# First attention of a three-part transformer kernel: fp32r scores, the bias added on VectorE, tables by sixteen small DMAs, and a value product moved behind two score jobs

## What is computed

```python
s_own = einsum('hqd,hkd->hqk', qm, k_own) * scale + tb_moba[:, rel_bucket(d_own)]
p     = masked_softmax(s_own, d_own >= 0)              # 8 heads
s_cmp = einsum('gjqd,gnd->gjqn', qn, k_cmp) * scale + tb_nsa[:, :, rel_bucket(d_cmp)]
s_s   = einsum('gjqd,gqnkd->gjqnk', qn, k_s) * scale + tb_nsa[...]   # selected
s_w   = einsum('gjqd,gkd->gjqk', qn, k_w) * scale + tb_nsa[...]      # window
o_b   = g0 * softmax(s_cmp) v_cmp + g1 * softmax(s_s) v_s + g2 * softmax(s_w) v_w
```

## Time and profile before

| | us |
|---|---|
| median of the timed runs (1383.39 to 1383.76) | 1383.43 |
| the profiled execution's own time | 1381.03 |
| its span, first to last instruction | 1379.2 |
| PE busy in the span | 1317.9 (96%) |
| DVE busy | 793.6 (58%) |
| ACT busy | 617.5 (45%) |
| POOL busy | 173.1 (13%) |
| mean granted clock of TensorE, share of full speed | 0.971 |

### The profile page before, as it was taken

One profiled execution on the slowest core, in us unless ns is written; L12 is line 12 of the kernel. 1 busy time (PEld: TensorE's weight loads), 2 busy tenths in 40 slices (PEclk: granted clock), 3 DMA queues, 4 the chain that ended last, 5 costly groups with the idle time before them and its releaser, 6 DMA issues.

```text
span 1379.2 us, 23104 instructions
## 1 busy us (share of the span) xinstructions
PE 1317.9 (96%) x9908; PEld 1226.2 (89%) x9908; DVE 793.6 (58%) x1062; ACT 617.5 (45%) x936; POOL 173.1 (13%) x224
## 2 busy tenths in 40 slices
PE   5999999999999999999999999998799888999997
PEld 5997669999999868999999999998797558999996
DVE  5745446555456465556454766547755765766643
ACT  5424445554333354554345444444544534544432
POOL 4000002110000001111011111010402401011101
PEclk8999999999999999999999999999999959999999
DMA  6571004555636502455544454563252006255461
GB/s 253 215 248 61 1 31 148 183 183 191 206 132 205 187 7 92 156 183 205 194 160 167 163 184 163 189 207 142 94 201 69 1 1 221 94 187 182 146 208 71
DMA packets 33494, 204.45 MB, mean 148 GB/s; under 512 B 3552, under 2 KB 5872, under 8 KB 13168
## 3 DMA queue, kind: packets, MB, share of 16 engines
q1 hardware_dynamic: 33392, 202.97, 42.8%
HBM read 201.89 MB, written 1.07 MB: 147 GB/s over the span
## 4 chain that ended last, share of the span: by engine, by line
PE 83%; DVE 7%; issue 6%; ACT 3%; POOL 1%; DMA 0%; SPq 0%; POOLq 0%; ACTq 0%; DVEq 0%
PE ps L614 22%; PE ps L615 22%; PE ps L616 22%; PE ps L884 3%; DVE wl L567 2%; PE ps L635 1%; PE ps L636 1%; PE ps L637 1%; PE ps L885 1%; PE ps L836 1%; PE ps L1280 1%; PE ps L1278 1%; POOL acc L699 1%; PE ps L2189 1%; ACT wh L559 1%
## 5 line engine op out<-in xcount | busy, mean ns | idle before, releaser
L567 DVE TENSOR_TENSOR wl<-raw,wh 128x2048 fp32r<-128x2048 f32 (+3 forms) x201 | 429.1, 2139 | 212.5 <-ACT wh L559 212.2
L614 PE MATMUL ps<-xh,wh 128*128 128x256 f32 x1712 | 492.1, 287 | 34.4 <-DVE xl L689 17.2
L615 PE MATMUL ps<-xl,wh 128*128 128x256 f32 x1712 | 489.8, 286 | 0.0
L616 PE MATMUL ps<-xh,wl 128*128 128x256 f32 x1712 | 489.5, 286 | 0.0
L559 ACT ACTIVATE wh<-raw 128x2048 fp32r<-128x2048 f32 (+3 forms) x201 | 357.3, 1782 | 208.6 <-PE ps L616 179.2
L614 PEld LDWEIGHTS ps<-xh,wh 128*128 128x128 f32 x1712 | 334.5, 195 | 37.3 <-issue 25.1
L615 PEld LDWEIGHTS ps<-xl,wh 128*128 128x128 f32 x1712 | 334.4, 195 | 0.0
L616 PEld LDWEIGHTS ps<-xh,wl 128*128 128x128 f32 x1712 | 334.2, 195 | 0.0
L614 PE MATMUL ps<-ah,wh 128*128 128x256 f32 x1088 | 309.6, 285 | 1.1 <-DVE wl L567 1.1
L615 PE MATMUL ps<-al,wh 128*128 128x256 f32 x1088 | 308.8, 284 | 0.0
L616 PE MATMUL ps<-ah,wl 128*128 128x256 f32 x1088 | 308.7, 284 | 0.0
(11 more groups left out here) (323 smaller groups left out, 1314.5 us busy)
## 6 DMA issues: line engine op xcount, KB each, us to landing
raw<-wstream SPq DMA_DIRECT2D x157, 1024.0 KB, 4.9
raw<-wstream SPq DMA_DIRECT2D x32, 704.0 KB, 4.1
raw<-wstream SPq DMA_DIRECT2D x8, 768.0 KB, 4.2
e_bt<-scratch SPq DMA_DIRECT2D x4, 512.0 KB, 6.6
raw<-wstream SPq DMA_DIRECT2D x2, 560.0 KB, 5.5
consts<-consts SPq DMA_DIRECT2D x1, 1025.0 KB, 9.9
raw<-wstream SPq DMA_DIRECT2D x4, 256.0 KB, 5.2
h<-xt SPq DMA_DIRECT2D x4, 256.0 KB, 5.8
```

The lines of the kernel that those rows point to most:

```text
L567: e.g.tensor_tensor(WL[q][:, 0:w], RAW[i % RAWN][:, 0:w], f32(WH[q][:, 0:w]), ALU.subtract).then_inc(S["lo"], 1)
L614: e.g.matmul(o, wh[:, sl], xh[:, cs], start=start, stop=False, skip_group_check=pair)
L615: e.g.matmul(o, wh[:, sl], xl[:, cs], start=False, stop=False, skip_group_check=pair)
L616: ins = e.g.matmul(o, wl[:, sl], xh[:, cs], start=False, stop=k == p.nk - 1, skip_group_check=pair)
```

## The change

- **Scores.** Queries and keys get the high and low fp32r halves that the weights have. VectorE drains a pair to fp32, ScalarE rounds it (`act_halves`), VectorE subtracts (`dve_low`), for seven pairs of 128x512. A score block becomes three fp32r matmuls for the first 128 queries and three for the second.
- **Bias.** The products with `flip` go. VectorE adds the table with a `tensor_tensor_reduce` that reads the scores in PSUM and the table in SBUF, writes the negated sum to `PB` and reduces it by the minimum (`dve_max_biased`); ScalarE's exponential reads `PB` (`act_exp_biased`). The scores of job i wait for the maximum of job i-3 instead of its exponentials. The compressed scores are fp32r products of 16 columns, and VectorE adds their bias.
- **Tables.** The row is written 16 times for each head (16x16x385 in DRAM), and sixteen DMAs of 16 partitions and eight heads each read it in the right order of queries: eight behind the query product `qn`, eight behind `ev0`.
- **Order.** The value product `ev1`, with its drains, and VectorE's gates and compressed weights (`dve_even_gates`) go behind the first two score jobs, on PE, ACT and DVE.

```diff
+        def dve_halves(p, full, dh, dl, at, n, by=None):
+            product = dve_to(p, full, n, by)
+            def drain(e, pair):
+                if pair:
+                    dve_low(e, full, dh, dl, at, pair - 1)
+                product(e, pair)
+            return drain
+        def dve_low(e, full, dh, dl, at, pair):
+            sl = slice(pair * 512, pair * 512 + 512)
+            e.wait_ge(S["qkh"], at + pair + 1)
+            e.g.tensor_tensor(dl[:, sl], full[:, sl], f32(dh[:, sl]), ALU.subtract).then_inc(S["qkl"], 1)
+        def act_halves(p, full, dh):
+            def drain(e, pair):
+                sl = slice(pair * 512, pair * 512 + 512)
+                e.wait(p.out[pair])
+                e.g.activation(dh[:, sl], full[:, sl], ACT.Copy).then_inc(S["qkh"], 1)
+            return drain
...
+        def dve_max_biased(e, A, i, first, second):
+            b, p = A.bank(i), PB[i % 4]
+            e.wait_ge(S["sc"], A.base + i + 1)
+            if i >= 4:
+                e.wait_ge(S["tp"], A.pv(i - 4) + 1)
+            e.g.tensor_tensor_reduce(p[:, 0:128], PS[b][:, 0:128], first, -1.0, 3e38, ALU.add, ALU.min, nm(i)[:, 0:1])
+            e.g.tensor_tensor_reduce(p[:, 128:384], PS[b][:, 128:384], second, -1.0, 3e38, ALU.add, ALU.min,
+                                     nm(i)[:, 1:2]).then_inc(S["mx"], 1)
...
+            for a in range(8):
+                src = bass.AP(scratch.tensor, 8 * half * 16 * 385 + 127 - 16 * a, [[384, 16], [16 * 385, 8], [1, 256]])
+                e.g.dma_start(e_bt[16 * a:16 * a + 16, hs].rearrange("p (h s) -> p h s", h=8), src).then_inc(S[f"bt{half}"], 16)
...
-            act_gemm(e, G["km"])
+            act_gemm(e, G["km"], drain=act_halves(G["km"], e_kmf, e_kmh))
...
-            dve_gemm(e, G["km"], 0, drain=dve_to(G["km"], e_km, 0))
+            dve_gemm(e, G["km"], 0, drain=dve_halves(G["km"], e_kmf, e_kmh, e_kml, 2, 0))
             for i, name in enumerate(("cmpk", "cmpv")):
                 p = G[name]
                 dve_gemm(e, p, 0)
+                if i == 0:
+                    dve_low(e, e_kmf, e_kmh, e_kml, 2, 1)
...
+            A = EVEN
+            for i in range(A.n + 4):
+                if i == 2:
+                    dve_even_gates(e)
...
-            pe_toks(e, G["ev1"], x_ready(0))
             A = EVEN
             for i in range(A.n + 3):
+                if i == 2:
+                    pe_toks(e, G["ev1"], x_ready(0))
...
+        def pe_even_scores(e, i):
+            A = EVEN
+            if i == 0:
+                e.wait_ge(S["row"], 1)
+                e.wait_ge(S["qkl"], 7)
+            if i >= 3:
+                e.wait_ge(S["mx"], i - 3 + 1)
...
+            for o, s, n in ((ps[:, 0:128], qt * T, 128), (ps[:, 128:384], qt * T + 128, 256)):
+                qs, ks = slice(s, s + 128), slice(kt * T, kt * T + n)
+                e.g.matmul(o, qh[p_, qs], kh[p_, ks], start=True, stop=False)
+                e.g.matmul(o, qh[p_, qs], kl[p_, ks], start=False, stop=False)
+                ins = e.g.matmul(o, ql[p_, qs], kh[p_, ks], start=False, stop=True)
+            ins.then_inc(S["sc"], 1)
```

More of the change, by code:

```diff
@@ L430, in build @@
         RS = place("rs", 16)
-        EPS = place("eps", 2)
+        EPS = NM[:, 8:10]
         CQ = place("cq", 144)
@@ L457, in build @@
         e_bt = place("e_bt", 16 * 256, at=rl)
+        ks_at = [rl[0], rl[0] + 4096]
+        e_ksf = nc.alloc_sbuf_tensor_at("e_ksf", [128, 2 * T], F32, offset=ks_at[0] + 2048)
+        e_ksh, e_ksl = (place(n, 2 * T, F32R, at=ks_at) for n in ("e_ksh", "e_ksl"))
         e_v = [place(f"e_v{i}", 792, at=m) for i in range(2)]
@@ L462, in build @@
         e_hs = [place("e_hs", 256, at=late), SMALL[:, 256:512]]
-        e_ht = place("e_ht", 2 * 30, at=ra)
+        e_ht = place("e_ht", 64, at=ra)
         e_hr = place("e_hr", 2 * 256, at=ra)
-        e_kc = place("e_kc", 32, at=ra)
+        e_kch, e_kcl = (place(n, 16, F32R, at=ra) for n in ("e_kch", "e_kcl"))
         e_vc = place("e_vc", 128, at=ra)
         e_pc = place("e_pc", 512, at=late)
-        e_ptc = [place(f"e_ptc{i}", 256, at=ra) for i in range(2)]
+        e_ptc = [place("e_ptc0", 256, at=m), place("e_ptc1", 256, at=ra)]
         ra, rl, m = *over(KT + 4), mid()
@@ L1017, in act_even @@
                 e.g.activation(pcv[:, tb, :, 0:15], pcv[:, tb, :, 0:15], ACT.Exp).then_inc(S["pce"], 1)
[L1018 to L1022, removed]
             A = EVEN
             for i in range(A.n + 3):
+                if i == 2:
+                    act_gemm(e, G["ev1"], drain=act_toks(G["ev1"], e_v, 512, 0))
+                    for tb in range(2):
+                        gz = e_v[tb][:, 768:792]
+                        e.wait_ge(*G["ev1"].out[tb])
+                        e.g.activation(gz, gz, ACT.Exp, scale=-1.0).then_inc(S["gz"], 1)
                 if i < A.n:
-                    act_exp(e, A, i)
+                    act_exp_biased(e, A, i)
                 if 0 <= i - 2 < A.n:
@@ L1112, in dve_even @@
             ins.then_inc(S["ev_dve"], 1)
[L1113 to L1117 removed]
+            dve_low(e, e_qnf, e_qnh, e_qnl, 4, 1)
+            dve_gemm(e, G["ks"], 0, drain=dve_halves(G["ks"], e_ksf, e_ksh, e_ksl, 6, 0))
+            p = G["kc"]
+            e.wait_ge(*p.end[0])
+            e.g.tensor_copy(e_kch[:, :], PS[p.bank[0]][:, 0:16]).then_inc(S["kch"], 1)
+            e.wait_ge(S["kch"], 1)
+            e.g.tensor_tensor(e_kcl[:, :], PS[p.bank[0]][:, 0:16], f32(e_kch[:, :]),
+                              ALU.subtract).then_inc(S["ev_dve"], 1)
+            p = G["vc"]
+            e.wait_ge(*p.end[0])
+            e.g.tensor_copy(e_vc[:, :], PS[p.bank[0]][:, 0:128]).then_inc(S["ev_dve"], 1)
+            dve_low(e, e_ksf, e_ksh, e_ksl, 6, 0)
             dve_gemm(e, G["ev0"], 0)
[L1119 removed]
+            nmx = SMALL[:, 0:16]
             e.wait_ge(S["zero"], 2)
+            e.wait_ge(S["bt1"], 128)
             for tb in range(2):
```

144 lines of the change are left out of this document (71 added, 73 removed).

## The result

The changed kernel takes 1406.83 us (median of 4 runs, 1404.15 to 1408.51) against 1383.41 us before (4 runs, 1381.88 to 1383.76). The ratio is 1.0172, with a 95% interval of 1.0159 to 1.0185: slower, by 23.4 us. Rival (A) of the prediction is what happened, the forecast of 1363.7 us is not. Some kernels of the experiments fall into two groups of executions some 40 us apart; there I give the executions one by one, because a median between the groups means nothing.

What follows compares the result with a forecast made beforehand. TensorE was taken to set the attention's pace. Scores -32.4, ev1 +1.1, waits +4.1, halves +5.0, low clock +2.5 gave -19.7 on 1381.03; with 2.4 for the median, 1363.7 us. Own range 1355 to 1371, with rivals 1355 to 1400.

Steps and rivals of the forecast that it cites:

- Rival (A): Attention jobs: the clock stays low until the output projection, +13.6 us, 1397 us, slower; chance 0.41.
- It falls: TensorE's granted clock falls in the new 4.3 us wait behind ev1, near the start of the attention jobs.
- It returns after about 6 us of jobs: Attention jobs: uninterrupted work brings the full clock back; until then jobs cost 3.24 instead of 1.92 us, +2.5 us.
- low-clock score block: Attention scores on TensorE at the low clock: estimated at 1.0 us a block, against 0.71 at the full clock.
- Scores at the full clock: Attention scores on TensorE: a block takes 0.71 us (0.54 to 0.74), a job 1.92 us; -32.4 us.
- The wait behind the gates: Second job's transposes: TensorE waits 4.3 us for weights VectorE makes after the gates, 0.2 before; +4.1 us.
- Second value product: ev1, with two score blocks ahead of it at the low clock: ends 1.1 us later, not 2.0.
- VectorE's maxima: Attention jobs: the new bias-and-reduce pair takes the old pair's duration, 0.55 us, at most 1.1; TensorE still leads.
- rival (D): Attention jobs: VectorE sets the pace because the new instruction runs at half rate, 1366 to 1368 us; 0.44 together with forecast.
- Halves: Front, query and key halves: their order on ScalarE and VectorE delays chunk 10's half, +5.0 us (3 to 7).
- Queues: SP's 16 table DMAs instead of four, ahead of weight chunks: both groups have over 15 us, so no cost.
- the low stretch: Start of the attention jobs: about 6 us at the low clock before it returns, +2.5 us (range 0 to 10 us).

Runs made afterwards that it cites:

- e2: Changed kernel, wait left in, plus 60 dummy fp32r products of 256 columns ahead of the ninth score job: 1380.43 us, ratio 0.9986.
- e11: Changed kernel, wait left in, plus 24 dummy fp32r products of 256 columns ahead of the ninth score job: 1376.52 us, ratio 0.9958.
- e5: Changed kernel plus 14 dummy products ahead of the fourth score job: 1365.35, 1364.12 and 1405.24, 1403.46 us.
- e6: Changed kernel with the order part undone exactly, compressed-weight transposes ahead of the fifth score job: 1367.56, 1368.0 and 1406.81, 1406.94 us.
- e1: Changed kernel plus 28 dummy fp32r products of 256 columns ahead of the fourth score job, filling the wait: 1362.92 us, ratio 0.9869.
- e3: Changed kernel with second value product and gates ahead of the jobs again, compressed-weight transposes ahead of the third job: 1404.79 us, ratio 1.0171.
- e10: Kernel before the change with only ev1 and the gates moved behind the first two score jobs: 1385.49 us, ratio 1.0034.
- e7: e4 with the halves of km moved behind the first compression: four executions of 1357.2 to 1359.2 us, one of 1399.7.
- e4: Changed kernel with VectorE's gates and compressed weights spread over later jobs, their transposes moved to job 10: 1362.51 us, ratio 0.9863.
- e8: e7 with the 48 compressed-score products spread between the first value product's blocks: 1366.16, 1365.21 and 1394.89, 1395.99, 1394.78, 1396.13 us.

## Why the prediction was wrong

**The clock: the step that failed.** "It falls" was right, and so was the place. "It returns after about 6 us of jobs" was wrong in this kernel: it took 89 us, and the four times agree with that. The step weighed the density of the stream and put the new jobs between `ev1`, which brought the clock back, and the last attention, which didn't. They behave like the last attention. Both of its premises were off: the 0.96 us of columns fill a block that takes 1.58 us, not 1.0, and the gap in the row of 1110 isn't at a weight load but at a wait for ScalarE (idle from 1119.4 to 1120.05 us, the only one there):

```profile
1120.05 1.08 PE L884 MATMUL ps<-pt,m_v 128*64 128x256 f32 x2 [0.64 <-ACT pt L855]
```

e2 and e11 show the difference: dense fp32r products bring it back in 2.5 us, and the jobs, at the same 10.00 of 10 us busy, hold it but seldom bring it back. The trace of after has the comparison twice: behind a wait of 3.10 us in the compressions (until 67.23 us) the clock fell too, and in the run of fp32r products of 256 columns that follows, it was back after 3.4 us (68.5 to 71.9); behind the wait of 3.13 us, in the jobs, it took 89. Keeping and regaining are two questions, and I asked one. The Trainium skill, page "TensorE: Matmul & The Clock Gate", Part 1, says that sustained activity releases the throttle; a row of 50.00 busy us in 50 at 0.50 speaks against reading "sustained" as busy. The same part of that page of the Trainium skill says that the chip's watching isn't tied to the kernel's start, so that the transition differs from run to run; the two groups of e5 and e6 would fit it, but no run here tests it.

**The size of rival A.** It said 1397 us. Its condition, a low clock until the output projection, was met to 4 us. Its term for a low-clock score block was 1.0 us; it is 1.58 (132.63 to 134.21). Products of 128 columns follow each other at 0.21 us there, no faster than those of 256 (133.86 less 133.65), as both do at 0.11 to 0.12 at the full clock. 20 blocks of 0.58 more are 11.6 us: 1408.6 against the measured 1406.8. The other terms held: transposes 0.82 for 0.77, value product 1.48 for 1.47.

**Scores at the full clock.** Forecast 0.71, measured 0.89 (135.39 to 136.28, e1). The 0.115 for 128 columns was right; missing were the start of each group (0.16 to 0.18 instead of 0.12) and 0.2 between the last product and the transposes. A job is 2.16 us for 1.92: 5.3 us over 22 jobs.

**The wait behind the gates.** Forecast 4.3, measured 3.13: the gates took the 2.75 us that before had shown, the low half ended 1.25 us behind `ev1` as before, not 2.0, and the cover was 2.3 us (120.26 to 122.57), not 1.84. And its place in the sum was wrong in kind: I charged the new order for it. e3 and e6, with the old order and the rest of the change, have waits of 2.98 and 4.94 us.

**Second value product.** Forecast +1.1 us. From the first compressed score to the end of `ev1` it is 15.3 us in after (104.99 to 120.26) and 14.6 before (98.99 to 113.61): +0.7. e10 shows that this hangs on where the clock comes back.

**VectorE's maxima.** From 124.26 to 124.81 the new pair takes 0.55 us, what the old pair took; rival (D) was wrong. Each is followed by an accumulator read of 0.08 us. The Trainium skill, page "VectorE: DVE Perf Modes", section "Two Vector instructions with no wait between them", tells of this second instruction; the trace agrees, and here it overlaps the next one (both start at 124.47), so it adds nothing to the pair.

**Halves.** Forecast +5.0 us for the order of the halves. Chunk 10's low half came 6.05 us later (72.23 for 66.18), but chunk 6's was 1.6 late already (53.40 for 51.81), ahead of km's halves; the order took 4.5. e7, with only that order changed against e4, gives 4.7 back: right in place and near in size. The two waits of TensorE on line 573 add up to 3.4 us, not 5, where one of 0.8 stood before; the fall of the clock behind the longer one, 3.4 us at 0.50, adds 1.7.

**Queues.** Nothing was forecast and nothing came: the tables landed in 6.8 us (before 6.6), and no wait names them.

The forecast's time itself stands in e4 (1362.5 for 1363.7): there the wait (4.1) and the low stretch (2.5) are gone and the bigger jobs (5.3) come on top, 1362.4 by the same sum. That these nearly cancel is luck. The sum was sound to some 5 us for a kernel that keeps the clock, and the chance of 0.41 for rival A was too low beside a row that showed a busy attention at 0.50.

## What to carry to other kernels

When a part of TensorE's work is made shorter, ask what it covered: first on the engines behind it (a chain of 4 us needs 4 us of cover), then for the clock, because a wait of 1.6 to 5 us in a stream of small mixed products may cost 40 us and not 3. Keep work that nobody needs soon (gates, weight halves of the next stage) out of the first iterations of a pipelined loop, and read the granted clock for every stage before and after. Repeat the execution several times: a kernel with such a wait can have two times.

## What the runs showed of the hardware

- After a fall the clock stayed at 0.50 for 89 us (after, e8) and 96 us (e3, e6), with TensorE busy all but a few microseconds at the start. Dense fp32r products of 256 columns with a 128-column operand brought it back after 2.4 and 2.5 us in the two traces, and all 18 executions show the gain. Where it came back without them, in five traces, TensorE had made transposes and value products for 3.3 us or more, and no score block.
- 48 fp32r products of 16 columns in a row, TensorE busy throughout, dropped the clock (0.71 in 109 to 110 us of after); spread between products of 512 columns they didn't (three traces).
- In the score blocks fp32r products of 128 and of 256 columns, each with a fresh operand over 64 rows, cost the same: 0.11 to 0.12 us apart at 1.00, 0.21 at 0.50.
- One kernel loses 30 to 40 us in some executions and little in others: 2 of 4 with a wait of 1.63 us in its trace, 4 of 6 with 2.23, 2 of 4 with 4.94, but 4 of 4 with 2.98 and with 3.13 us. How often doesn't follow from the wait's length alone.
